# Up projections of a two-layer decoder trunk: the products with high weights first, those with low weights last

## The reference

```python
def conv_ffn(h, w_up, conv_w, conv_b, w_down):
    u = h @ w_up                                  # (256 x 1024) @ (1024 x 5632)
    up = jnp.pad(u, ((0, 0), (CONV_WIDTH - 1, 0), (0, 0)))
    c = conv_b
    for tap in range(CONV_WIDTH):                 # causal depthwise conv, width 3
        c = c + conv_w[tap] * up[:, tap:tap + S]
    gate, val = jnp.split(c, 2, axis=-1)
    return (jax.nn.gelu(gate, approximate=True) * val) @ w_down
```

## Time and profile before

| | |
|---|---|
| median of 3 runs | 675.29 us |
| the profiled execution | 675.03 us |
| its span, first to last instruction | 673.2 us |
| TensorE busy | 656.9 us (98%) |
| VectorE busy | 459.7 us (68%) |
| ScalarE busy | 381.6 us (57%) |
| GpSimd busy | 156.8 us (23%) |
| mean granted clock of TensorE | 0.999 of full |

### The profile page before, as it was taken

One profiled execution on the slowest core, in us unless ns is written; L12 is line 12 of the kernel. 1 busy time (PEld: TensorE's weight loads), 2 busy tenths in 40 slices (PEclk: granted clock), 3 DMA queues, 4 the chain that ended last, 5 costly groups with the idle time before them and its releaser, 6 DMA issues.

```text
span 673.2 us, 10262 instructions
## 1 busy us (share of the span) xinstructions
PE 656.9 (98%) x3732; PEld 548.1 (81%) x3732; DVE 459.7 (68%) x621; ACT 381.6 (57%) x547; POOL 156.8 (23%) x123
## 2 busy tenths in 40 slices
PE   7999999899999999999999999999999999999996
PEld 5888877577788888888887999777788888888885
DVE  5597777785777878876457645576777878786532
ACT  6646444775665757575345533575467676667320
POOL 0321310000034343432001000490123434344000
PEclk9999999999999999999999999999999999999999
DMA  8976633005254545455652664303354353644601
GB/s 306 407 253 248 245 126 126 1 2 188 76 237 174 200 165 208 163 212 226 221 197 107 250 226 150 126 1 138 119 211 189 136 238 139 233 135 185 245 0 62
DMA packets 18651, 115.61 MB, mean 172 GB/s; under 512 B 2591, under 2 KB 3133, under 8 KB 5693
## 3 DMA queue, kind: packets, MB, share of 16 engines
q1 hardware_dynamic: 17469, 111.52, 44.2%
q10 hardware_dynamic: 1152, 3.67, 1.5%
HBM read 114.14 MB, written 1.05 MB: 171 GB/s over the span
## 4 chain that ended last, share of the span: by engine, by line
PE 89%; DVE 3%; ACT 2%; issue 2%; DMA 1%; POOL 1%; SPq 0%; DVEq 0%; POOLq 0%; ACTq 0%
PE ps L1715 22%; PE ps L1272 13%; PE ps L1274 13%; PE ps L1273 13%; PE ps L1717 11%; PE ps L1314 4%; DMA raw<-in_weights 1%; PE ps L1494 1%; PE ps L1614 1%; PE ps L1766 1%; PE ps L1755 1%; PE ps L1267 1%; PE ps L1472 1%; POOL rstd L1181 1%; PE ps L1540 1%
## 5 line engine op out<-in xcount | busy, mean ns | idle before, releaser
L700 DVE TENSOR_TENSOR wlo<-raw,whi 128x2048 fp32r<-128x2048 f32 x99 | 225.8, 2313 | 66.0 <-ACT whi L360 66.0
L360 ACT CAST whi<-raw 128x2048 fp32r<-128x2048 f32 x99 | 186.2, 1919 | 72.7 <-PE ps L1274 65.8
L1715 PE MATMUL ps<-xpair,whi 128*128 128x512 f32 x640 | 226.4, 399 | 0.0
L1717 PE MATMUL ps<-xpair,wlo 128*128 128x256 f32 x640 | 179.8, 281 | 0.0
L1715 PEld LDWEIGHTS ps<-xpair,whi 128*128 128x128 f32 x640 | 120.3, 188 | 29.9
L1717 PEld LDWEIGHTS ps<-xpair,wlo 128*128 128x128 f32 x640 | 120.9, 189 | 0.0
L1227 POOL TENSOR_TENSOR hidf<-act_g,conv 128x512 f32<-128x512 f32 x22 | 73.9, 3357 | 83.9 <-ACT act_g L604 83.9
L1272 PE MATMUL ps<-whi,hid_hi 128*128 128x512 f32 x176 | 69.4, 394 | 0.0
L1274 PE MATMUL ps<-whi,hid_lo 128*128 128x512 f32 x176 | 69.0, 392 | 0.0
L1272 PE MATMUL ps<-whi,xpair 128*128 128x512 f32 x168 | 67.5, 402 | 1.0 <-DVE pcm L932 0.8
L1273 PE MATMUL ps<-wlo,hid_hi 128*128 128x512 f32 x176 | 68.3, 388 | 0.0
(11 more groups left out here) (193 smaller groups left out, 969.9 us busy)
## 6 DMA issues: line engine op xcount, KB each, us to landing
raw<-in_weights SPq DMA_DIRECT2D x101, 1024.0 KB, 4.9
c_gpost<-in_gpost ACTq DMA_DIRECT2D x4, 512.0 KB, 4.9
raw<-in_weights SPq DMA_DIRECT2D x3, 512.0 KB, 9.1
c_gpre<-in_gpre ACTq DMA_DIRECT2D x3, 512.0 KB, 4.2
h<-in_x SPq DMA_DIRECT2D x2, 512.0 KB, 5.7
out<-h SPq DMA_DIRECT2D x4, 256.0 KB, 2.0
raw<-in_weights SPq DMA_DIRECT2D x2, 256.0 KB, 5.7
t<-in_masks SPq DMA_DIRECT2D x1, 512.0 KB, 12.5
```

The costliest lines, as they stand in the source:

```text
L360: act.copy(whi[:, slot, :], raw[:, slot, :]).then_inc(hi_done, 1)
L700: dve.tensor_tensor(wlo[:, slot, :], raw[:, slot, :], whi[:, slot, :].bitcast(F32), ALU.subtract).then_inc(lo_done, 1)
L1715: pe.matmul(ps[:, b0 + m, :], whi[:, slot, cols], xpair[:, kt].rearrange("p a c -> p (a c)"), start=kt == 0, stop=kt == KT - 1, skip_group ...
L1717: ins = pe.matmul(ps[:, b0 + m, 0:SEQ], wlo[:, slot, cols], xhi[:, kt, :], start=False, stop=kt == KT - 1, skip_group_check=True)
```

## The change

`up_chunk` runs the 16 products with high weights of a half first, over all four m and four b, and then the 16 with low weights. The wait for `lo_done` moves between the two groups, and a wait for `hi_done` of the same unit stands ahead of the first. The products, their operands, their destinations, the order of m and b in each group and the place of `unit_used` (with the last product of the half) are the same.

```diff
                     for half in range(2):
                         slot = slots[half]
+                        blocks = [(m, b, slice(b * BLK + m * P, b * BLK + (m + 1) * P)) for m in range(4) for b in range(4)]
+                        pe.wait_ge(hi_done, at[half] + 1)
+                        for m, b, cols in blocks:
+                            kt = 4 * half + b
+                            pe.matmul(ps[:, b0 + m, :], whi[:, slot, cols], xpair[:, kt].rearrange("p a c -> p (a c)"),
+                                      start=kt == 0, stop=kt == KT - 1, skip_group_check=True)
                         pe.wait_ge(lo_done, at[half] + 1)
-                        for m in range(4):
-                            for b in range(4):
-                                kt = 4 * half + b
-                                cols = slice(b * BLK + m * P, b * BLK + (m + 1) * P)
-                                pe.matmul(ps[:, b0 + m, :], whi[:, slot, cols], xpair[:, kt].rearrange("p a c -> p (a c)"),
-                                          start=kt == 0, stop=kt == KT - 1, skip_group_check=True)
-                                ins = pe.matmul(ps[:, b0 + m, 0:SEQ], wlo[:, slot, cols], xhi[:, kt, :], start=False,
-                                                stop=kt == KT - 1, skip_group_check=True)
+                        for m, b, cols in blocks:
+                            kt = 4 * half + b
+                            ins = pe.matmul(ps[:, b0 + m, 0:SEQ], wlo[:, slot, cols], xhi[:, kt, :], start=False,
+                                            stop=kt == KT - 1, skip_group_check=True)
                         ins.then_inc(unit_used, 1)
```

## The result

The changed kernel runs in 671.38 us (median of 6 runs, 670.35 to 672.91), the kernel before in 675.29 us (6 runs, 674.56 to 677.43). The ratio is 0.9938, 95% interval 0.9921 to 0.9954: 3.9 us faster, where 3.5 us were forecast.

A forecast was written before the change was run, and what follows sets the result against it. TensorE's dense stream of products was taken as the bound. A half falls from 5.654 us to 5.562 plus 0.005, 0.087 us less, times 40 halves 3.5 us: 675.29 - 3.5 = 671.8 us, range 670.4 to 676.5.

The forecast's parts named there:

- That TensorE's stream is the bound and its waits cost nothing: Up loops and down projections: one dense stream of products on TensorE; existing, moved and added waits put at 0 us.
- rival C: Middle of a half: the moved wait stops loads being pulled ahead, up to 0.19 us a half, at most 679.3 us; chance 0.05.
- One sign of being wrong: Trace after the change: the forecast is wrong if, among other signs, a stage outside the loops changes its length.
- The wide product at 0.2275 us: Up loops: each 512-column product, in runs of 16, takes 0.2275 us; ends 0.2265 and 0.236, today's distance in the pair.
- The narrow product at 0.1201: Up loops: each 256-column product, in runs of 16, takes 0.1201 us instead of 0.117, a loss of about 3 ns.
- The two changes of kind at 5 ns a half: Each half: switching wide to narrow and back adds 0.005 us together, the rounding of one start.
- Rival A: Up loops: order does not matter, the 5.8 ns belong to the operands; wide product 0.233 us, time 675.3 us; chance 0.19.
- Rival B: Up loops: narrow runs become load-bound, 0.117 to 0.1201 us, wide products stay at 0.236; 677.3 us; chance 0.13.

The follow-up runs named there:

- two_waits: The kernel before, wide and narrow products still in turn, with a wait for hi_done added ahead of the wait for lo_done: 674.74 us against 675.86, ratio 0.998.
- one_wait: The changed kernel with the old single wait for lo_done at the head of each half, none for hi_done: 672.93 us, ratio 0.9954 to the kernel before.
- both_512: The kernel before, products still in turn, with the narrow product made 512 columns wide: loops of 144.96 us against 113.03.

## Why the prediction was right

**That TensorE's stream is the bound and its waits cost nothing**: right. No start at a boundary was late before, the new wait added nothing (`two_waits`), the later wait for the low split won nothing (`one_wait`), and rival C, a bubble behind the 16th wide product, is refuted by 226 or 227 ns at that place. One sign of being wrong did show, a stage outside the loops that changed its length (the attention, 1.5 us); it went with the granted clock of that profile, and in the second profile of the same kernel it was gone.

**The wide product at 0.2275 us**: the runs hold it when settled (226.7 ns), but in each the first five take longer, so that 16 take 16 x 226.7 + 27 = 3.654 us, where 3.640 were forecast. **The narrow product at 0.1201**: 120 when settled, the first is 113; 16 take 1.913 us, where 1.922 were forecast. **The two changes of kind at 5 ns a half**: nothing at the change itself, and 27 ns behind it. I took the price from single starts, 0.22 and 0.11 us, which stand at the change, while it falls on the five products that follow. It could have been read in the trace of before, right behind those rows: from 43.84 to 45.01 us the five wide products behind the narrow run start 234, 236, 228, 232 and 231 ns apart. The three errors (14 ns too little, 9 and 5 too much) cancel: a half was put at 5.567 us and measured 5.567, the loops at 3.5 us less and measured 3.46. That the sum came out this close is luck in part. The stated range, 670.4 to 676.5 us, held no change too; it is the trace of the loops, and not the median inside the range, that decides against rivals A and B.

**Rival A** (the order does not matter) had for it that one change from wide to narrow shows no price in its own start. `both_512` answers it: the same operands, xpair as moving side and strided weight blocks, run at 226.7 ns when the lengths are equal. The formula of the Trainium skill that stood beside it ("TensorE: Matmul & The Clock Gate", section "Back-to-back issue gap": columns / 2.4 + 2.5 ns) has the product's own columns alone in it, and this case does not agree: the same product of 512 columns cost 236 ns between narrow ones and 227 in a run. The prediction also left out what that section of the Trainium skill says of its formula: it is the gap of an isolated product, while in a stream both the loads and the products set the spacing, at about 131 ns for 512 columns. No stream here comes near that figure; the settled ones take 226.7 ns. **Rival B** (narrow runs bound by their loads): its own half is true, the narrow product rose from 117.1 to 119.5 ns in the mean, and its load's record from 189 to 192; but the wide one fell from 236.2 to 228.4. That the load is what sets the 120 was not tested by itself.

What the prediction lacked was the mechanism: it added rates of homogeneous streams, which gave the right sum, and did not say why the mixture costs more. The runs show a disturbance at the start of a stream, and that products of unlike length in turn keep paying for it. What in the chip makes it was not found.

## What to carry to other kernels

Where TensorE is the bound and its products differ in length, keep products of one length together, in runs long against five: here 16 in a run won 5.4 ns a pair and 4 in a run about 2.9 (1.9 us over 640 pairs). Read such an effect from start to start in the trace, stage by stage; the median of some runs, which lie 2 to 5 us apart, would not have told the variants from each other. And look at the settled rate of each dense stream: one that runs at 228.9 where others run at 226.7 is worth a look at where its tiles lie. When two loops end with different kinds of product, read both to the first product behind them.

## What the runs showed of the hardware that was not expected

- A dense stream of 512-column products starts slowly: behind a narrow run about 233, 236, 228, 233 and 231 ns, then 226.7 for as long as it lasts, over waits that are already met, changes of ring slot, bank and weight tile. After idle time it takes 5 to 11 products to settle. In the stretches at half the granted clock this does not happen; the products start 426 or 427 ns apart.
- Alternating 512 with 256 columns costs for as long as it lasts: 353.3 ns a pair against 346.7 for settled products. 512 with 384 gives 406.7, against 400 by an estimate.
- The place in SBUF of the tiles that were moved matters by 1%: 228.9 ns a product with the tile 320 bytes past a multiple of 512, 226.7 with it 128 bytes past. Only this one shift was tried, and it moved the tiles behind (`conv`, `act_g`, `hidf`) along with the hidden ones, so which boundary counts, and whether the weight side alone makes it, stays open.
- The granted clock dropped to 0.72 over 6 us of the attention stage in one profile and not in another of the same kernel, at the cost of some 1.5 us. TensorE had been busy for 4.6 of the 6 us in both.
